# Sample convolution of a hybrid decoder step moved from TensorE to GpSimd and VectorE

## What is computed

```python
u = ua * jax.nn.sigmoid(ub)                      # 512 channels, prompt and samples
full = jnp.concatenate([hist, u], axis=1)        # samples: 30 rows of state_conv ahead of 8 new ones
c = lax.conv_general_dilated(full, w_dw[:, None, :], (1,), 'VALID',
                             dimension_numbers=('NWC', 'WIO', 'NWC'),
                             feature_group_count=CONV_CH) + b_dw        # depthwise, width 31
c = layernorm(c, ln_g, ln_b); c = c * jax.nn.sigmoid(c)
_, idx = lax.top_k(score, 256)                   # the search below finds its threshold bit by bit
m = concat(attn_out, c) @ w_out                  # then norms and the MLP
```

## Time and profile before

| what | us |
|---|---|
| median of three runs | 1568.24 (1567.1 to 1569.48) |
| the profiled execution | 1569.07 |
| its span in the trace | 1566.9 |
| `phase_select` in the trace, first and last | 208.85 to 452.40 |
| of it the search, until the last tiny operation (L1216) | 217.70 to 377.7 |
| TensorE's granted clock over the span | 0.992 |

### The profile page before, as it was taken

One profiled execution on the slowest core, in us unless ns is written; L12 is line 12 of the kernel. 1 busy time (PEld: TensorE's weight loads), 2 busy tenths in 40 slices (PEclk: granted clock), 3 DMA queues, 4 the chain that ended last, 5 costly groups with the idle time before them and its releaser, 6 DMA issues.

```text
span 1566.9 us, 22129 instructions
## 1 busy us (share of the span) xinstructions
PE 1497.9 (96%) x8490; PEld 1255.5 (80%) x8490; DVE 678.9 (43%) x1322; ACT 603.9 (39%) x1081; POOL 439.1 (28%) x451
## 2 busy tenths in 40 slices
PE   7998999999899998899999999999999999999995
PEld 4466356654788764478799999999999999999995
DVE  2438467878935564435532222222222222222234
ACT  4217549886447765644331221212112021120211
POOL 3233014442613433423321121121122112112124
PEclk9999999999999999999999999999999999999998
DMA  7021141447481006340021111111111111111112
GB/s 241 1 59 58 49 90 76 164 120 97 173 260 63 2 9 257 139 155 1 1 62 47 41 43 52 40 40 54 40 40 42 52 40 42 52 40 40 55 41 101
DMA packets 95635, 116.65 MB, mean 74 GB/s; under 512 B 15142, under 2 KB 80758, under 8 KB 92996
## 3 DMA queue, kind: packets, MB, share of 16 engines
q1 hardware_dynamic: 92076, 94.72, 20.1%
q0 software_dynamic: 3488, 20.98, 3.6%
HBM read 95.05 MB, written 20.95 MB: 74 GB/s over the span
## 4 chain that ended last, share of the span: by engine, by line
PE 55%; POOL 1%; DVE 1%; DMA 0%; issue 0%; ACT 0%; DVEq 0%; POOLq 0%; ACTq 0%
PE ps L2375 18%; PE ps L2377 18%; PE ps L2376 18%; PE ps L2410 0%; POOL y L2270 0%; DVE y L2545 0%; DMA out_y_p<-y 0%; POOL wlo L2234 0%; PE ps L2462 0%; DVE y L2555 0%; POOL stat L2245 0%; ACT whi L2284 0%; ACT hhi L2342 0%; POOL stat L2241 0%; DVEq L2544 0%
## 5 line engine op out<-in xcount | busy, mean ns | idle before, releaser
L2234 POOL TENSOR_TENSOR wlo<-wraw,whi 128x1024 fp32r<-128x1024 f32 x62 | 149.0, 2403 | 566.4 <-ACT whi L2284 566.3
L2376 PE MATMUL ps<-xlo,whi 128*128 128x384 f32 (+1 forms) x768 | 250.3, 326 | 0.0
L2375 PE MATMUL ps<-hhi,whi 128*128 128x384 f32 (+1 forms) x720 | 235.1, 327 | 0.8 <-POOL wlo L2234 0.8
L2377 PE MATMUL ps<-hhi,wlo 128*128 128x384 f32 (+1 forms) x720 | 235.2, 327 | 0.0
L2376 PE MATMUL ps<-hlo,whi 128*128 128x384 f32 (+1 forms) x720 | 234.9, 326 | 0.0
L2284 ACT CAST whi<-wraw 128x1024 fp32r<-128x1024 f32 x62 | 65.2, 1052 | 293.8 <-PE ps L2377 293.8
L2522 DVE TENSOR_TENSOR rel<-rel 128x384 f32<-128x384 f32 (+1 forms) x96 | 51.5, 537 | 283.7 <-ACT rel L2350 283.7
L2350 ACT ACTIVATE rel<-ps 128x384 f32<-128x384 f32 (+1 forms) x96 | 45.3, 473 | 264.3 <-PE ps L2377 264.3
L2376 PEld LDWEIGHTS ps<-xlo,whi 128*128 128x128 f32 x768 | 144.1, 188 | 0.0
L2375 PEld LDWEIGHTS ps<-hhi,whi 128*128 128x128 f32 x720 | 135.2, 188 | 1.1 <-POOL wlo L2234 1.1
L2377 PEld LDWEIGHTS ps<-hhi,wlo 128*128 128x128 f32 x720 | 135.1, 188 | 0.0
(11 more groups left out here) (316 smaller groups left out, 2795.7 us busy)
## 6 DMA issues: line engine op xcount, KB each, us to landing
wraw<-in_w_up SPq DMA_DIRECT2D x32, 512.0 KB, 4.0
wraw<-in_w_down SPq DMA_DIRECT2D x32, 512.0 KB, 3.4
taps<-qT SPq DMA_DIRECT2D x9, 960.0 KB, 4.0
hT<-taps SPq DMA_DIRECT2D x7, 960.0 KB, 4.9
x<-in_x SPq DMA_DIRECT2D x13, 512.0 KB, 7.3
w<-in_w_u SPq DMA_DIRECT2D x2, 2048.0 KB, 8.0
wo_raw<-in_w_out SPq DMA_DIRECT2D x8, 512.0 KB, 4.2
out_y_p<-y SPq DMA_DIRECT2D x8, 512.0 KB, 2.6
```

Source lines behind the costliest of these rows:

```text
L2234: nc.gpsimd.tensor_tensor(wlo_of(j, last), raw[:], whi_of(j, last), ALU.subtract).then_inc(s_wlo, 1)
L2375: nc.tensor.matmul(o, wh, xh, start=first, stop=False)
L2376: nc.tensor.matmul(o, wh, xl, start=False, stop=False)
L2377: return nc.tensor.matmul(o, wl, xh, start=False, stop=last)
```

## The change

- The samples no longer go through `by_channel`, `up` and TensorE. `up` holds the prompt alone: 132 columns in, XO = 128 out; a convolution matmul has 128 moving columns, and four groups fill a bank (8 banks instead of 11). `take_conv` is one copy a bank.
- `usm` now holds each sample's 30 + 8 rows in plain order (128 x 4 x 8 x 38). ScalarE's history copy is one operation for each half, GpSimd no longer clears `usm`.
- For each channel group c GpSimd multiplies, in two halves of four samples, every window of 31 rows by the 31 taps (`multiply_sample`, 992 products a partition, two operations for a group). It does so right behind the diagonals of the unit that brought the new tokens (units 2, 5, 8, 11).
- VectorE sums them: two `tensor_reduce` (992 to 32) behind its counts of bits 7, 13, 19 and 25, ahead of its wait for ScalarE. The sums go to `ysm` in the room that `up` leaves free; ScalarE copies them into `conv` in one operation behind the copies of the keys.
- SP loads the taps once more in plain order (`dwn`), and no longer stores `usm`. The wait on `s_iw` ahead of the ties goes.

The diff, cut to what the prediction speaks of:

```diff
-XRUN = XT - XS + 1
-XO = T // PH
+XT = (HIST + 2 + SEQ) // PH
+XO = SEQ // PH
-CONV_BANK = 3
+CONV_BANK = 4
+    reduce_at = {7 + 6 * c: c for c in range(CC)}
...
+            def multiply_sample(c):
+
+                for h in range(2):
+                    if c >= 1:
+                        pool.wait_ge(s_ys, N_YS + 2 * c + h - 1)
+                    x = usm[:, c, h * HB:(h + 1) * HB, 0:NT]
+                    window = bass.AP(x.tensor, x.offset, list(x.ap) + [[1, CW]])
+                    taps_of = dwn[:, c, :].unsqueeze(1).unsqueeze(1).broadcast_to([P, HB, NT, CW])
+                    nc.gpsimd.tensor_tensor(prods[h].rearrange("p (b t j) -> p b t j", b=HB, t=NT), window, taps_of,
+                                            ALU.mult).then_inc(s_pr, 1)
...
                     for j, g in enumerate(range(*SAVE[q - 1])):
                         diagonal(g, made[:, (q - 1) % 2, j * WN:(j + 1) * WN])
+                if wp < w:
+                    pool.wait_ge(s_te, HEV)
+                    pool.wait_ge(s_un, c + 1)
+                    multiply_sample(c)
...
-                dst = usm[:, :, :, e * hb * XS:(e + 1) * hb * XS].rearrange("p c s (b x) -> p c b x s", x=XS)
-                nc.scalar.copy(dst[:, :, :, 0, 2:PH], src[:, :, :, 0:PH - 2])
-                for c in range(CC):
-                    last = nc.scalar.copy(dst[:, c, :, 1:XS - 1, :],
-                                          src[:, c, :, PH - 2:HIST].rearrange("p b (x s) -> p b x s", s=PH))
-                last.then_inc(s_te, 1)
+                nc.scalar.copy(usm[:, :, e * hb:(e + 1) * hb, 0:HIST], src).then_inc(s_te, 1)
...
+            act.wait_ge(s_iw, 16 * 2)
+            nc.scalar.copy(conv.rearrange("p c (o x) -> p c x o", o=PH)[:, :, XO:, :],
+                           ysm.rearrange("p c (b t) -> p c b t", t=NT))
...
-                        last = nc.tensor.matmul(o, wdiag[g][:, j * P:(j + 1) * P], up[:, g, j:j + XRUN],
+                        last = nc.tensor.matmul(o, wdiag[g][:, j * P:(j + 1) * P], up[:, g, j:j + XO],
...
                 count_all(dve_sets, cand, ALU.is_ge)
+                if it in reduce_at:
+                    for h in range(2):
+                        dve.wait_ge(s_pr, N_PR + 2 * reduce_at[it] + h + 1)
+                        nc.vector.tensor_reduce(ysm[:, reduce_at[it], h * HB * NT:(h + 1) * HB * NT],
+                                                prods[h].rearrange("p (n j) -> p n j", j=CW), AX_X, ALU.add
+                                                ).then_inc(s_ys, 1)
                 dve.wait_ge(s_cnt, it + 2)
                 dve.wait_ge(s_acnt, it + 1)
```

More of the change, by code:

```diff
@@ L155, in build @@
             m["mask"] = sb_in(qkv, "mask", [P, MK_COLS], BF16)
-            m["up"] = sb_in(qkv, "up", [P, NCG, XT])
+            up = sb_in(qkv, "up", [P, NCG * UP_ROOM])
+            m["up"] = up[:, 0:NCG * XT].rearrange("p (g x) -> p g x", x=XT)
+            m["up_rest"] = up[:, NCG * XT:]
             m["kT"] = sb_in(qkv, "kT", [P, T])
@@ L697, in phase_select @@
     conv = moT[:, CC:KC, :]
-    upr = conv.rearrange("p c t -> p (c t)")[:, 0:CC * PH * XP].rearrange("p (c s x) -> p c s x", c=CC, s=PH)
-    usm = sb_in(st, "usm", [P, CC, PH, NB * XS])
+    upr = conv.rearrange("p c t -> p (c t)")[:, 0:CC * PH * XT].rearrange("p (c s x) -> p c s x", c=CC, s=PH)
+    usm = sb_in(st, "usm", [P, CC, NB, HIST + NT])
+    dwn = sb_in(st, "dwn", [P, CC, CW])
+    HB = NB // 2
+    ysm = m["up_rest"][:, 0:CC * NB * NT].rearrange("p (c n) -> p c n", c=CC)
     wq = wslot[0]
@@ L725, in phase_select @@
     z = sb_in(st, "zq", [P, 3, QC])
+    prods = [m["up_rest"][:, CC * NB * NT:CC * NB * NT + HB * NT * CW],
+             z[:, 1:3, :].rearrange("p a n -> p (a n)")[:, 0:HB * NT * CW]]
     rt = sb_in(st, "rtq", [P, 2, 4, NH * HALF])
@@ L745, in phase_select @@
     tie = [used[:, KEYS:KEYS + KEYS // 2].bitcast(BF16),
-           usm[:].rearrange("p c s x -> p (c s x)")[:, 0:KEYS // 2].bitcast(BF16)]
+           usm[:].rearrange("p c b x -> p (c b x)")[:, 0:KEYS // 2].bitcast(BF16)]
     sets = [(P, scores[:, SC_OFF[i]:SC_OFF[i] + P * (i + 1)], mask[:, MK_OFF[i]:MK_OFF[i] + P * (i + 1)])
@@ L755, in phase_select @@
     s_fetch, N_FETCH = m["p_x"], [16 * 4, 16 * 3, 16 * 2]
+    s_pr, N_PR = m["p_first"], 16 * 3
+    s_ys, N_YS = m["p_const"], 16 * 6
     s_h = sem("s_h")
@@ L879, in _ @@
                 sp.wait_ge(s_um, len(uunits) // 2 * (h + 1))
[L880 to L883, removed]
+                sp.dma_start(by_channel[:, cs2, :, :], upr[:, cs2, :, :]).then_inc(s_iw, 16)
+                sp.wait_ge(s_iw, 16 * (h + 1))
                 for c in range(2 * h, 2 * h + 2):
@@ L937, in _ @@
                     pool.wait_ge(s_um, q + 1)
-                    nc.gpsimd.tensor_copy(usm[:, c, :, :].rearrange("p s (b x) -> p b s x", x=XS)[:, :, :, XS - 1],
+                    nc.gpsimd.tensor_copy(usm[:, c, :, HIST:HIST + NT],
                                           unew[:, c, :].rearrange("p (b t) -> p b t", t=NT)).then_inc(s_un, 1)
@@ L1018, in take_conv @@
                 act.wait_ge(s_cg, g0 + ng)
-                src = bank[2 + EVENTS.index(("c", k)) % 6][:, 0:CONV_BANK * XRUN].rearrange("p (g x) -> p g x", x=XRUN)[:, 0:ng, :]
-                nc.scalar.copy(up[:, g0:g0 + ng, 0:SEQ // PH], src[:, :, 0:SEQ // PH])
-                late = src[:, :, SEQ // PH:].rearrange("p g (b x) -> p g b x", x=XS)[:, :, :, XS - 1]
-                nc.scalar.copy(up[:, g0:g0 + ng, SEQ // PH:XO], late).then_inc(s_ce, 1)
+                nc.scalar.copy(up[:, g0:g0 + ng, 0:XO],
+                               bank[2 + EVENTS.index(("c", k)) % 6].rearrange("p (g x) -> p g x", x=XO)[:, 0:ng, :]
+                               ).then_inc(s_ce, 1)
             for it in range(BITS):
@@ L1147, in convolve @@
                         pe.wait_ge(s_fetch[n % 3], N_FETCH[n % 3] + 16 * (n // 3 + 1))
-                    o = bank[2 + e % 6][:, (g % CONV_BANK) * XRUN:(g % CONV_BANK + 1) * XRUN]
+                    o = bank[2 + e % 6][:, (g % CONV_BANK) * XO:(g % CONV_BANK + 1) * XO]
                     for j in range(STEPS):
-                        last = nc.tensor.matmul(o, wdiag[g][:, j * P:(j + 1) * P], up[:, g, j:j + XRUN],
+                        last = nc.tensor.matmul(o, wdiag[g][:, j * P:(j + 1) * P], up[:, g, j:j + XO],
                                                 start=(j == 0), stop=(j == STEPS - 1))
@@ L1256, in _ @@
             dve.wait_ge(s_u, len(uunits))
-            dve.wait_ge(s_iw, 16 * 4)
             for q, j in enumerate(TIE_ORDER):
```

23 lines of the change are left out of this document (11 added, 12 removed).

## The result

The changed kernel takes 1591.43 us (median of four runs, 1589.99 to 1592.13), the kernel before 1567.67 us beside it: 1.015 times as long, with a 95% interval of 1.013 to 1.017. The profiled execution took 1592.13 us with a span of 1590.3. The prediction was 1588 us, slower.

A forecast was written before the change was run, and what follows sets the result against it. The search in `phase_select` was taken to lead, TensorE following with 2 us of slack. 1569.07 + 28.7 for the longer search - 9.5 for the shorter convolution = 1588.3 profiled, so a median of 1588 us; range 1572 to 1598.

The forecast's parts named there:

- The path: In `phase_select` the search leads, TensorE follows with 2 us of slack; at the other end SP is late next.
- The products: GpSimd's products, 2.0 us each, hold VectorE's tiny steps `keep` and `v_bits` behind a unit: bit 7's candidate 3.6 us later.
- The sums: VectorE's two reduces of a group take 1.25 us each; by themselves they cost 1.6 us in each of four bits.
- Step 3: Sums push VectorE's tiny steps into the next unit's GpSimd diagonals: +4.3 us from candidate 7 to 9.
- Three groups: Products and sums of the first three channel groups lengthen the search by 7.9 us a group, 23.7 in all.
- Unit 11: Last group, bits 24 and 25: products ahead of the diagonals cost 3.4 us, the sums 1.6, together 5.0.
- The search: The bit search in `phase_select` gets longer by 28.7 us, 23.7 plus 5.0.
- a few tenths: ScalarE's ten history copies becoming two in bit 4 can only help, by a few tenths; counted as nothing.
- The tail: Behind the last turn, 160 matmul records at 0.110 us instead of 200; next block 9.5 us earlier, SP last.
- tiny steps slip through: Rival: each train of GpSimd work holds up one VectorE tiny step, not three; search +16.3 us, 1575 us; chance 0.12.
- nothing excludes: Rival: no exclusion between products and tiny steps, only the sums cost; -2.9 us, 1565.3 us, faster; chance 0.12.

The follow-up runs named there:

- e2: e1 with GpSimd's products waiting for VectorE's next candidate, so that they run beside the counts; 1564.64 us, 0.9985 of the kernel before.
- e4: Changed kernel with each product replaced by three GpSimd writes of zeros, about as long together; 1574.68 us, 1.005 of the kernel before.
- e1: Changed kernel with VectorE's sums one bit later (bits 8, 14, 20, 26); 1581.12 us, 1.009 of the kernel before.
- e5: Changed kernel without products and without sums, the samples' convolution left out; 1559.48 us, 0.993 of the kernel before.
- e3: e2 with the two sums of a group in two bits (8 and 10, and so on; last 25 and 26); 1561.27 us, 0.996 of the kernel before.
- e9: e3 with each unit's third diagonal held until the next odd bit's candidate and a group's products behind different candidates (unit 11's both in 25); 1558.41 us, 0.994 of the kernel before.
- e10: Kernel before with only the third diagonal of every unit waiting for the candidate of the next odd bit; 1565.83 us, 0.999 of the kernel before.
- e6: Changed kernel without the products, the sums kept in place over zeros; 1574.69 us, 1.004 of the kernel before.
- e7: Changed kernel without the sums, the products kept in place; 1577.79 us, 1.006 of the kernel before.
- e8: Changed kernel with each product cut into four pieces, one sample each, at the same place; 1581.0 us, 1.007 of the kernel before.

## Why the prediction was right, step by step

- **The path** was read rightly: the search leads, TensorE follows, and at the other end SP is late next. The copy of `hist` ends at 408.8 (predicted: near 407; 1.8 us of it come from ahead of the block), and SP's last issue ends last.
- **The products**: 2.0 us predicted, 2.12 to 2.17 measured, `keep` and `v_bits` at 2.05 and 2.04 in bit 6. Candidate 6 to 7 takes 9.46 us instead of 5.71: +3.75, predicted +3.6. In the next two groups it is +3.85 and +3.81. e2 takes the cost away by position alone, e4 by taking the reads away.
- **The sums**: 1.25 us each predicted, measured 1.10 from one to the next and 1.18 alone. In a free bit the two cost 1.24 us behind the 0.86 of waiting, where 1.6 was predicted.
- **Step 3**: +4.3 predicted, and candidate 9 at +14.55 from candidate 7 to the hundredth. That exactness has luck in it, since shorter sums and longer products offset each other. e1 removes this step alone: from candidate 7 to 9 it takes 11.14 us there (258.64 to 269.78), +0.93 instead of +4.34, and three times the difference are the 10.2 us by which its search is shorter.
- **Three groups** cost 8.1 to 8.2 us each, predicted 7.9. **Unit 11**: 5.0 predicted. Measured from candidate 24 to 26 it was 15.64 us, where bit 24 took 5.69 before and a clean bit 4.95: +5.0.
- **The search** in sum: +29.0 against +28.7. Products and sums alone make 29.4 (over e5). The other 0.4 came back where the prediction had put "a few tenths" at nothing: with two history copies instead of ten, bit 5 took 4.95 us instead of 5.35.
- **The tail**: -8.7 against -9.5. All of the gain lies behind the last turn, as predicted. The pace is 18.13 / 160 = 0.113 us, predicted 0.110. The stores begin 8.8 us after the first of those records (predicted 8.2), and the next block begins 0.68 us behind SP's last issue (predicted 0.4): that is the 0.8 us, but for 0.1. Between them luck was at work: the stores took 9.04 us and the last issue 0.65, where the prediction carried over 7.97 and 0.34, but the last store was followed by the last issue after 1.66 us and not 3.17, so the three together came to 11.35 us instead of 11.48.
- **The rest**: the median is 3.4 us above the forecast, the span 4.2 above the sum. Search and tail make 1.1 of that, 1.8 lies in `phase_project`, which has two lengths in these profiles, and 1.2 behind the block. The changed code explains neither of the last two, and the runs don't tell why.
- **The rivals**: that tiny steps slip through is refuted by five rows of the kernel after, one GpSimd operation for each tiny step (2.05, 2.04, and 1.20 three times). That nothing excludes is refuted by e2 against e1.

e3 and e5 have tails of 61.9 and 61.8 us, 12.7 below the kernel before. That isn't a larger gain of the shorter convolution. Behind the last turn the kernel before takes 29.57 us (422.87 to 452.44), and the ten kernels with the shorter convolution take 20.3 to 21.3: 8.3 to 9.3 us of gain, predicted 9.5. The other 3.5 to 3.6 us of e3 and e5 lie ahead of that turn, and the last section says where.

## What to carry to other kernels

Before moving work to an engine that is half idle, ask whether its operations and those of an engine on the critical path exclude each other: there a chain of tiny dependent steps waits for one whole operation at each step. Put such work behind a signal that the other engine has entered work that isn't held up (here: the next candidate is written and the counts follow), or cut it into pieces. And when the path gets shorter, ask what leads next: e9 and e10 each cut the search by some 4 us more, and TensorE's own work took the lead after 2.

## What the runs showed of the hardware

**The exclusion** holds between a VectorE operation with two SBUF inputs and a GpSimd operation that reads SBUF. It holds for the whole operation (2.05 us for a product of 2.12, 0.59 for a piece of 0.64, 1.20 for a diagonal of 1.25), in both directions (e9's rotations), and not against a GpSimd write (0.17 us) or for a reduce (1.18 us inside a diagonal, in e1). When both engines have such operations waiting they alternate, one whole operation each.

**TensorE's clock** I hadn't weighed at all. The view is the table of windows (stretch in us; busy time and instructions of TensorE's matmuls, its weight loads, VectorE, ScalarE, GpSimd; granted clock; DMA share; GB/s), first of the kernel after, then of the kernel before, then of e3:

```profile
396.00:402.00 6.00, 0.00 (x0) 0.00 (x0) 5.00 (x15) 5.55 (x8) 1.79 (x6) 0.71 0.00 0
402.00:408.00 6.00, 0.00 (x0) 0.00 (x0) 4.14 (x15) 5.09 (x9) 0.00 (x0) 0.50 0.00 0
410.00:412.00 2.00, 2.00 (x6) 1.27 (x5) 1.83 (x7) 1.93 (x4) 0.78 (x3) 0.50 0.29 55
412.00:414.00 2.00, 2.00 (x6) 0.78 (x5) 2.00 (x3) 0.12 (x1) 1.84 (x8) 0.95 0.02 4
...
380.00:382.00 2.00, 2.00 (x3) 0.67 (x2) 2.00 (x5) 0.79 (x2) 1.84 (x7) 0.50 0.19 33
...
380.00:382.00 2.00, 2.00 (x6) 0.90 (x5) 1.96 (x4) 0.99 (x3) 1.76 (x7) 1.00 0.23 44
```

After the change TensorE is idle for 13.19 us. The granted clock falls to 0.50 (1.2 instead of 2.4 GHz) in that time. The work begins again at 408.84, and the clock is still 0.50 from 410 to 412 and 0.95 from 412 to 414. The turns take 1.97 us instead of 1.09. From the turns to the start of q block 8 it is 9.96 us (408.84 to 418.80), and 8.33 in e3 (378.16 to 386.49): 1.6 us for the clock.

The delay then grows. From the first turns to that of q block 6 it is 32.0 to 32.1 us in all eight kernels in whose profile the clock fell (before, after, e1, e2, e4, e6, e7, e8), and 29.1 and 29.2 in e3 and e5, where it didn't: 3.0 us. The rows suggest why: in e3 the rotation of block 6 starts at 395.34, ahead of the long scan of the ties (396.13), and after the change at 427.65, behind its start (426.71), so its first step waits for the scan. In e9 it starts behind it too (393.20 against 392.54), without a fall of the clock, and lasts 13.5 us instead of 11.9. No run tests this by itself. The rest of the 4 us by which the tail of e3 is shorter than that of the kernel after is 0.7 in the banks behind that turn and 0.3 at the end. Against the kernel before, whose clock fell too, it is the same 3.0 us, 0.6 in the banks, and 9.1 behind the last turn. So the clock is no part of the 29.0 and -8.7 us by which the change moved search and tail; it is what a kernel with a short wait can win.

What decides whether it falls stays open. In the kernel before 2.04 us of idle time were followed by the fall, in e3 2.20 us and in e5 1.65 us were not. Waits of 5.76 us (e2) to 13.19 us always were. Nor is it the same in every execution. Of the 46 executions of the kernel before that were timed beside the experiments, eight had a granted clock of 0.995 or 0.996 over the span and took 1563.6 to 1564.5 us, and the other 38 had 0.989 to 0.994 and took 1565.5 to 1573.4. Where in the span their clocks differed isn't on record. So a difference of 3 us between two single profiles can be the clock alone.
